# The activations h and the arena 32 bytes further on in the partition

## The reference

```
x = x + 0.5 * swiglu(rms_norm(x, ffn1_norm[l]), w_gate[l], w_up[l], w_down[l])
h = rms_norm(x, mix_norm[l]);  a, g, q, k, v = split(h @ w_in[l])
x = x + concat([conv_module(a, g, ...), diff_attention(q, k, v, ...)]) @ w_out[l]
x = x + 0.5 * swiglu(rms_norm(x, ffn2_norm[l]), ...)
# second block
x = x + g1 * (retention_mixer(h, ...) or sgu_mixer(h, ...))
x = x + g2 * peer_ffn(h, w_query[l], sub_keys[l], expert_u[l], expert_v[l])
```

## Time and profile before

| | us |
|---|---|
| median of 3 runs | 3121.96 (3120.95 to 3129.87) |
| the profiled execution, its own time | 3121.82 |
| span of that profile | 3120.0 |

### The profile page before, as it was taken

How to read it: one execution, slowest core, us unless ns; L and a number is a source line. 1 busy time by engine, 2 the same in 40 slices (tenths; PEclk the granted TensorE clock), 3 DMA queues, 4 the chain that set the end, 5 groups by cost and what they waited for, 6 DMA issues and landing times.

```text
span 3120.0 us, 53574 instructions
## 1 busy us (share of the span) xinstructions
PE 3052.1 (98%) x22724; PEld 2879.1 (92%) x22724; DVE 2174.6 (70%) x3454; ACT 1622.8 (52%) x2437; POOL 188.0 (6%) x155
## 2 busy tenths in 40 slices
PE   8999999999999999999999999999999999999999
PEld 8998999999899989999999998878989998999887
DVE  5867786876787645799655556765758985555666
ACT  5565554565544455456544445556444564444454
POOL 0000000000000000740000000000038000000000
PEclk9999999999999999999999999999999999999999
DMA  6762576775277544447866657645445587666663
GB/s 236 261 232 105 192 268 238 273 254 182 83 262 263 176 163 149 161 177 269 295 218 216 215 205 247 209 169 189 162 151 188 214 301 242 216 217 215 223 237 122
DMA packets 153262, 654.63 MB, mean 210 GB/s; under 512 B 10332, under 2 KB 77472, under 8 KB 78272
## 3 DMA queue, kind: packets, MB, share of 16 engines
q1 hardware_dynamic: 96576, 584.09, 52.5%
q10 hardware_dynamic: 56032, 65.66, 6.2%
q0 software_dynamic: 416, 1.45, 0.1%
HBM read 616.55 MB, written 34.61 MB: 209 GB/s over the span
## 4 chain that ended last, share of the span: by engine, by line
PE 88%; DVE 7%; ACT 3%; POOL 1%; issue 1%; DMA 0%; ACTq 0%; DVEq 0%
PE ps L588 19%; PE ps L589 19%; PE ps L590 19%; PE ps L593 8%; PE ps L594 8%; PE ps L595 8%; PE ps L1009 2%; DVE w_lo L1513 2%; PE ps L747 2%; ACT w_hi L1078 1%; POOL w_lo L2092 1%; PE ps L656 1%; DVE raw L1508 0%; DVE at L1981 0%; DVE at L1985 0%
## 5 line engine op out<-in xcount | busy, mean ns | idle before, releaser
L1513 DVE TENSOR_TENSOR w_lo<-raw,w_hi 128x1024 fp32r<-128x1024 f32 x932 | 1135.2, 1224 | 624.7 <-ACT w_hi L1078 623.2
L1078 ACT ACTIVATE w_hi<-raw 128x1024 fp32r<-128x1024 f32 x1000 | 1051.4, 1055 | 698.5 <-PE ps L590 450.0
L588 PE MATMUL ps<-h_hi,w_hi 128*128 128x256 f32 x4224 | 1185.7, 281 | 16.0 <-DVE w_lo L1513 10.1
L589 PE MATMUL ps<-h_lo,w_hi 128*128 128x256 f32 x4224 | 1176.7, 279 | 0.0
L590 PE MATMUL ps<-h_hi,w_lo 128*128 128x256 f32 x4224 | 1176.4, 278 | 0.0
L588 PEld LDWEIGHTS ps<-h_hi,w_hi 128*128 128x128 f32 x4224 | 796.7, 189 | 22.0 <-issue 10.8
L590 PEld LDWEIGHTS ps<-h_hi,w_lo 128*128 128x128 f32 x4224 | 801.3, 190 | 0.0
L589 PEld LDWEIGHTS ps<-h_lo,w_hi 128*128 128x128 f32 x4224 | 796.4, 189 | 2.8 <-issue 0.2
L593 PE MATMUL ps<-w_hi,at 128*128 128x512 f32 x1024 | 398.5, 389 | 3.1 <-DVE at L2038 3.1
L595 PE MATMUL ps<-w_hi,at 128*128 128x512 f32 x1024 | 398.4, 389 | 0.0
L594 PE MATMUL ps<-w_lo,at 128*128 128x512 f32 x1024 | 398.3, 389 | 0.0
(11 more groups left out here) (275 smaller groups left out, 3105.3 us busy)
## 6 DMA issues: line engine op xcount, KB each, us to landing
raw<-in_peer_u SPq DMA_DIRECT2D x128, 1024.0 KB, 4.8
raw<-in_peer_v SPq DMA_DIRECT2D x128, 1024.0 KB, 4.8
raw<-in_ffn_gu SPq DMA_DIRECT2D x88, 1024.0 KB, 4.9
raw<-in_ada_w SPq DMA_DIRECT2D x48, 1024.0 KB, 5.0
raw<-in_ffn_down SPq DMA_DIRECT2D x44, 1024.0 KB, 4.9
gates<-at ACTq DMA_DIRECT2D x32, 1024.0 KB, 5.3
at<-gates ACTq DMA_DIRECT2D x24, 1024.0 KB, 6.0
raw<-in_w_in SPq DMA_DIRECT2D x16, 1024.0 KB, 4.9
```

What stands on the lines that cost most here:

```text
L588: e.matmul(o, lhs[0], rhs[0], start=start, stop=False)
L589: e.matmul(o, lhs[0], rhs[1], start=False, stop=False)
L1078: e.activation(whi[:, u % NPAIR, :], raw(k, half), ACT.Copy).then_inc(hi_done.hit(u), 1)
L1513: e.tensor_tensor(wlo[:, m % NPAIR, :], raw(k, half), whi[:, m % NPAIR, :].bitcast(FP), ALU.subtract).then_inc(w_lo_dve.hit(m), 1)
```

## The change

`rcol` is moved from behind `rr` to in front of `h_hi`. With its 32 bytes it pushes `h_hi`, `h_lo` and the small tensors up to `rr` 32 bytes on; everything from `mod` on, the weight tiles among it, stays where it was. The arena starts at 160 instead of 128 modulo 512. In the PEER stage the gap in front of `p_hi` shrinks from 64 to 32 bytes, so that `p_hi`, `p_lo` and what follows them stay where they were; `R` moves with the arena. No instruction is added, removed or moved in any engine's order.

```
         x = sb("x", [128, KT, T])
+        rcol = sb("rcol", [128, 2])
         hh_ = sb("h_hi", [128, KT, T], FR)
...
         rr = sb("rr", [128, T])
-        rcol = sb("rcol", [128, 2])
...
-        arena_at = (nc.sbuf_base + 511) // 512 * 512 + 128
+        arena_at = (nc.sbuf_base + 511) // 512 * 512 + 160
...
         R = carve(NRING, T)
-        carve(16)
+        carve(8)
         p_hi = [carve(T, dt=FR) for _ in range(4)]
```

## The result

The changed kernel takes 3164.14 us (median of 4 runs, 3162.9 to 3164.49) against 3121.45 us (4 runs, 3117.53 to 3129.87): a ratio of 1.0128, 95% interval 1.0112 to 1.0145. It is slower by 42.7 us where 31 us less were forecast. It lies at the time of the rival "inside the slow region", all long steps, 3161 us, and 0.1 us above the stated range.

A forecast was written before the change was run, and what follows sets the result against it. TensorE was taken to bound the kernel, through slow steps between matmuls in dense stretches. 3121.8 - 31.5 (those steps made fast) - 0.5 (`project_rows`) + 0.5 (new VectorE waits) = 3090.3; forecast 3090 us, range 3084 to 3164 us.

The forecast's parts named there:

- inside the slow region: Rival (34%): same stall in all dense stretches; all slow 3161 us (24%), larger stall in each matmul up to 3216 us (10%).
- What bounds the kernel: TensorE, clock granted in full in every slice; dense 256-column steps of 113.3 or 117.9 ns, the slow state entered after interruptions.
- The cost of the new distance: 256-column matmuls, h or arena moving, 32 bytes in front: bounds -31.5 to +94 us; lower end taken, all fast.
- `project_rows`: Its 576 matmuls go from 64 to 32 bytes behind: -0.5 us taken, -1.9 at best, +1.5 at worst.
- The v products at 0: PEER stage, 3072 products of 512 columns: both addresses kept, so 0 us change.
- New waits on VectorE (+0.5 us): The split on VectorE is late next when TensorE gets 4% faster in the slow stretches; 0.5 us added.
- The two read ports: Under rival "the distance does not matter" (19%, 3122 us): TensorE reads moving operand and weight load independently, waiting for no one.
- The phase that the prediction speaks of: Dense stretches: weight load starts some 3 ns behind the matmul, reads collide, one stalls the other, and the stall keeps the phase.

## Why the prediction was wrong

- What bounds the kernel was right: TensorE's steps, two of them for one instruction, and a fall into one or the other at an interruption. The trace before shows both, and the experiments with the small tensors and p show the second as a cause: moving tensors, among them what the interrupting matmuls read, changed the step behind them. One reading was too strong: a 9 in the clock row means 90% or more, and the mean granted clock is 0.991 before and 0.992 after, not full in every slice.
- "The cost of the new distance" is the step that failed: "I take the lower end. The new distance lies between 0, where no stall is seen, and 64, which is at the edge". Neither end bears it. The 389 ns at distance 0 are of matmuls with 512 moving columns, where a weight load has 226.7 ns to be done instead of 113.3; with 256 columns distance 0 takes 120.0 ns, the longest of all together with 256. And 64 is no edge: 48 and 80 are at 119.2 and 119.3 ns. I took one class of matmuls for another and a single good place for the border of a region.
- The rival "inside the slow region" has the time, 3161 us, but in part by luck. Its price, +39 us, is 4.5 ns on some 8,700 short steps. The new step is not the old long one: it is 118.3 ns, not 117.8, on all 16,200 dense steps, another 8 us, and `project_rows` and the v products add 5.5. The 12 us of waits and half clock that went the other way were not in that price either.
- `project_rows` was expected at -0.5 us within -1.9 to +1.5; it cost 2.5 us, outside these ends.
- The v products at 0: they cost 3 us, though both addresses are unchanged. What was missed is that a stretch leaves its mark on the next one, here on nine matmuls; that it is a phase which is handed on is not shown.
- New waits on VectorE (+0.5 us): the reverse came, as TensorE got slower.
- The two read ports of the Trainium skill's page "SBUF — State Buffer" ("Who interferes with whom"), by which distance would not matter, do not cover this: the kernel with the weights 32 bytes nearer has the same instructions and the same place of h, and takes 1.24% longer. Here the measurement decides.

Open is why. The runs show that the matmul's step depends on the distance of the two starts, in 9 places, but not which part of the memory or of the engine the two streams meet in, why 64 is the good one, or whether the distances between the tried ones hide another. 0 and 256 give the same step to 0.1 ns and 128 another, so the pattern may repeat after 256 bytes; no run tried 64 + 256. The phase that the prediction speaks of is not to be seen in the records: a weight load starts 3.3 ns behind its matmul on the mean in short stretches and in long ones of the kernel before. Which of `sq`, `ones`, `ident` and `rcol` makes the difference behind `sums` and the other small products was not separated either.

## What to carry to other kernels

Where TensorE is bound by dense pairs of weight load and matmul, take the start times of consecutive matmuls and look for two steps of one instruction; the relative place of the two operands was worth 6% of the step here (113.3 against 120.0 ns) and 2% of the kernel (3111 against 3182 us), and it has to be measured for each shape, since what is good for 512 columns was the worst for 256. Don't carry a good distance to a neighbouring one: 16 bytes lost it. And where a stretch has two steady steps, look at what runs just before it.

## What was not expected of the hardware

- The same fp32r matmul of 128 x 256 takes 113.3 to 120.0 ns from start to start, at a granted clock of 1.00, by the distance of its operands and, at 64, by what ran before; the best 512-column one takes 226.7 ns, twice the 113.3.
- The small tensors from `sq` to `rr`, moved by 32 bytes (`sums` has 2.0 us of 30 in the stage shown), are worth 0.36% of the whole kernel.
- Kernels with h and the arena at a distance of 64 tend to scatter more from run to run (standard deviation 2.3 to 4.8 us, five to 23 runs each) than those with h at others (0.4 to 2.2 us, four runs each). That the moment of an interruption has a say there would fit, but with one execution of each recorded it is not shown.
